# Experts' weights loaded in pairs of chunks, 2 MB at a time, for the 41st to the 180th chunk of each layer

## What is computed

```python
def moe(x, w_router, b_router, w1, w3, w2):      # per layer; 16 experts, top 2 of one group
    e_idx, gates = route(xf, w_router, b_router)
    ...
    def expert_block(args):
        xb, e = args
        hb = jax.nn.silu(xb @ w1[e]) * (xb @ w3[e])
        return hb @ w2[e]                        # w1, w3, w2: [2 layers, 16, 1024, 1024] float32
```

## Time and profile before

| | us |
|---|---|
| Median of 3 runs (1787.92 to 1788.83) | 1788.22 |
| Span of the profiled execution | 1787.6 |
| PE busy (share of the span) | 1720.1 (96%) |
| DVE busy | 790.6 (44%) |
| ACT busy | 624.1 (35%) |
| Queue of the weights, share of 16 DMA engines | 75.9% |
| Chain that ended last: PE, DMA | 71%, 17% |
| DMAs issued, all queues together (the view of DMA issues, added up) | 529 in number |

### The profile page before, as it was taken

The page is one execution under the profiler, slowest core; times in us unless marked ns, Lnnn a source line. Parts: engine busy times, 40 slices in busy tenths (PEclk is TensorE's granted clock), DMA queues, the critical chain, the costliest instruction groups (busy, mean ns, idle before and its releaser), DMA issues.

```text
span 1787.6 us, 24011 instructions
## 1 busy us (share of the span) xinstructions
PE 1720.1 (96%) x10024; PEld 1114.5 (62%) x10024; DVE 790.6 (44%) x1510; ACT 624.1 (35%) x1197; POOL 121.0 (7%) x143
## 2 busy tenths in 40 slices
PE   9999999999899989999999989999999999999998
PEld 8974344433234974444333333887999899789986
DVE  6961111111003782111111011866888677768875
ACT  5541110000002661000000001666666564656664
POOL 0000000000000000000000000131111001401100
PEclk9999999999999999999999999999999999999999
DMA  9569999999999779999999999543555544435550
GB/s 390 236 249 409 423 424 423 422 422 421 419 421 419 279 298 391 423 423 424 422 422 421 419 420 420 194 141 120 188 189 177 199 159 150 141 120 179 186 189 24
DMA packets 76100, 544.91 MB, mean 305 GB/s; under 512 B 8528, under 2 KB 8528, under 8 KB 10576
## 3 DMA queue, kind: packets, MB, share of 16 engines
q1 hardware_dynamic: 75600, 542.15, 75.9%
q10 hardware_dynamic: 384, 1.13, 0.2%
HBM read 542.19 MB, written 1.05 MB: 304 GB/s over the span
## 4 chain that ended last, share of the span: by engine, by line
PE 71%; DMA 17%; DVE 7%; ACT 3%; issue 1%; POOL 1%; SPq 0%; DVEq 0%; ACTq 0%
PE PS L1112 25%; DMA ring<-in_w 17%; PE PS L383 12%; PE PS L385 11%; PE PS L384 11%; PE PS L1092 2%; PE PS L1166 2%; DVE wl L366 2%; PE PS L834 1%; PE PS L593 1%; ACT wh L360 1%; PE PS L1128 1%; PE PS L1180 1%; PE PS L1275 0%; DVE F L969 0%
## 5 line engine op out<-in xcount | busy, mean ns | idle before, releaser
L1112 PE MATMUL PS<-ring,F 128*64 128x512 f32 x1992 | 454.4, 597 | 30.4 <-DMA ring<-in_w 22.8
L366 DVE TENSOR_TENSOR wl<-ring,wh 128x512 fp32r<-128x512 f32 x504 | 363.6, 740 | 167.7 <-ACT wh L360 165.1
L360 ACT ACTIVATE wh<-ring 128x512 fp32r<-128x512 f32 x504 | 314.5, 631 | 273.6 <-PE PS L385 257.6
L383 PE MATMUL PS<-xh,wl 128*128 128x256 f32 x1168 | 336.5, 288 | 2.4 <-DVE wl L366 2.3
L1112 PEld LDWEIGHTS PS<-ring,F 128*64 128x64 f32 x1992 | 136.9, 137 | 322.4 <-issue 252.6
L384 PE MATMUL PS<-xl,wh 128*128 128x256 f32 x1168 | 330.4, 283 | 0.0
L385 PE MATMUL PS<-xh,wh 128*128 128x256 f32 x1168 | 330.3, 283 | 0.0
L383 PEld LDWEIGHTS PS<-xh,wl 128*128 128x128 f32 x1168 | 223.9, 192 | 5.6 <-DVE wl L366 2.7
L384 PEld LDWEIGHTS PS<-xl,wh 128*128 128x128 f32 x1168 | 223.9, 192 | 0.6
L385 PEld LDWEIGHTS PS<-xh,wh 128*128 128x128 f32 x1168 | 223.9, 192 | 0.0
L383 PE MATMUL PS<-wh,xl 128*128 128x512 f32 x352 | 142.5, 405 | 6.4 <-DVE xl L500 3.5
(11 more groups left out here) (393 smaller groups left out, 1905.0 us busy)
## 6 DMA issues: line engine op xcount, KB each, us to landing
ring<-in_w SPq DMA_DIRECT2D x255, 1024.0 KB, 26.6
F<-in_w SPq DMA_DIRECT2D x56, 1024.0 KB, 23.1
ring<-in_ffn_up SPq DMA_DIRECT2D x44, 1024.0 KB, 4.9
early<-in_w SPq DMA_DIRECT2D x40, 1024.0 KB, 24.4
ring<-in_ffn_down SPq DMA_DIRECT2D x22, 1024.0 KB, 4.9
Z<-in_w SPq DMA_DIRECT2D x21, 1024.0 KB, 26.7
XT<-in_w SPq DMA_DIRECT2D x10, 1024.0 KB, 24.2
ring<-in_even_w_in SPq DMA_DIRECT2D x9, 1024.0 KB, 19.7
```

The source lines that it names most:

```text
L360: act.e.activation(self.wh[:, p % NPIECE, :], self.piece_source(p), ACT.Copy).then_inc(*self.up("w_hi", p))
L366: dve.e.tensor_tensor(self.wl[:, p % NPIECE, :], self.piece_source(p), f32(self.wh[:, p % NPIECE, :]), ALU.subtract).then_inc(*self.up("w_ ...
L383: e.matmul(out, left[1], right[0], start=first, stop=False)
L1112: t = pe.e.matmul(PS[64 * half:64 * half + 64, bank, :], lhs(k), weights[:, a:a + 512], start=(k == 0), stop=(k == 7))
```

## The change

Expert loads at positions 40 to 179 of a layer are made two chunks at a time: one DMA of 128 rows of 16 KB (2 MB) into two slots that lie side by side. To allow it:

- slots are dealt in fixed pairs there: six pairs of the ring, (13, 12) and (15, 14) in F, (17, 18) and (19, 20) in `early`, and (Z, XT), for which Z and XT become one buffer. Up to chunk 127 that is 11 pairs, 22 slots; from 128 to 179 the six pairs of the ring, 12 slots. The pair whose younger chunk is the oldest is taken;
- SP waits for the release of both old chunks before it issues; both new chunks count as landed with the one DMA's semaphore;
- in HBM the four chunks of a matrix are laid side by side, [128, 8192], so that two neighbouring chunks are one run of 16 KB a partition. A single chunk is then 128 rows of 8 KB, 32 KB apart.

Chunks 0 to 39 and 180 to 191 of a layer are loaded singly as before, and so is every other weight.

```diff
+GROUPS = {2: [(i, i + 1) for i in range(0, RING, 2)] + [(13, 12), (15, 14), (17, 18), (19, 20), (Z_SLOT, XT_SLOT)]}
+FIRST_OF, SIZE = [], {}
+def _load_size(i):
+    return 2 if 40 <= i < 180 else 1
+def _oldest(groups, last):
+    return min(groups, key=lambda g: max(-1 if last[x] is None else last[x] for x in g))
...
     for position, n in enumerate(LOAD_ORDER):
-        slots = [*range(RING), Z_SLOT] if n < CHUNK["aq0"] else list(range(SMALL_RING))
-        slot = None
+        if SLOT[n] is not None:
+            continue
+        slots, size, group = [*range(RING), Z_SLOT] if n < CHUNK["aq0"] else list(range(SMALL_RING)), 1, None
...
+            size = _load_size(i)
             if i < len(FIRST_SLOTS[layer]):
-                slot = FIRST_SLOTS[layer][i]
+                group = FIRST_SLOTS[layer][i] and (FIRST_SLOTS[layer][i],)
             elif i < 128:
                 slots += [*F_SLOTS, *SPLIT_SLOTS, XT_SLOT]
-        if slot is None:
-            slot = min(slots, key=lambda x: -1 if last[x] is None else last[x])
-        SLOT[n], PREVIOUS[n] = slot, last[slot]
-        last[slot] = n
-        loads[slot] += n > 0
-        LOADS[n] = loads[slot]
+        if group is None:
+            group = _oldest([g for g in GROUPS[size] if set(g) <= set(slots)] if size > 1 else [(x,) for x in slots], last)
+        SIZE[n] = size
+        loads[group[0]] += n > 0
+        for m, slot in enumerate(group, n):
+            assert LOAD_ORDER[position + m - n] == m
+            SLOT[m], PREVIOUS[m], FIRST_OF[m] = slot, last[slot], n
+            LOADS[m] = loads[group[0]]
+            last[slot] = m
...
-        self.Z = sb("Z", [128, NT, D])
-        self.XT = sb("XT", [128, KD, T])
+        self.ZX = sb("ZX", [128, 2 * CH])
+        self.Z = self.ZX[:, 0:CH].rearrange("p (h d) -> p h d", h=NT)
+        self.XT = self.ZX[:, CH:2 * CH].rearrange("p (k t) -> p k t", k=KD)
...
-            return A[("w1", "w3", "w2")[i // 4 % 3]][int(name[3]), i // 12, i % 4]
+            c = i % 4 * CH
+            return A[("w1", "w3", "w2")[i // 4 % 3]][int(name[3]), i // 12, :, c:c + SIZE[n] * CH]
...
     def landed(self, n):
-        return self.ring_sems[SLOT[n]], 16 * LOADS[n]
+        return self.ring_sems[SLOT[FIRST_OF[n]]], 16 * LOADS[n]
...
+            if FIRST_OF[n] != n:
+                continue
             if KIND[n] == "expert" and SLOT[n] >= RING:
                 sp.wait_ge(*self.extra_free(n))
-            if PREVIOUS[n] is not None:
-                sp.wait_ge(self.released(PREVIOUS[n]))
+            for m in range(n, n + SIZE[n]):
+                if PREVIOUS[m] is not None:
+                    sp.wait_ge(self.released(PREVIOUS[m]))
...
-                sp.e.dma_start(self.chunk(n)[:, 0:src.shape[-1]], src).then_inc(self.ring_sems[SLOT[n]], 16)
+                sp.e.dma_start(self.chunk(n, SIZE[n])[:, 0:src.shape[-1]], src).then_inc(self.ring_sems[SLOT[n]], 16)
...
-        a[k] = c(w.reshape(2, 16, 4, 2, 128, 1024).transpose(0, 1, 2, 4, 3, 5).reshape(2, 16, 4, 128, 2048))
-    by_columns = i["moe_w2"][:, 15].reshape(2, 2, 4, 128, 2, 512).transpose(0, 4, 1, 3, 2, 5).reshape(2, 4, 128, 2048)
+        a[k] = c(i[n].reshape(2, 16, 8, 128, 1024).transpose(0, 1, 3, 2, 4).reshape(2, 16, 128, 8192))
+    by_columns = i["moe_w2"][:, 15].reshape(2, 2, 4, 128, 2, 512).transpose(0, 3, 4, 1, 2, 5).reshape(2, 128, 8192)
```

More of the change, by code:

```diff
@@ L128, in _place_stream @@
     last, loads = [None] * (RING + EXTRA), [0] * (RING + EXTRA)
-    SLOT.extend([None] * len(KIND))
-    PREVIOUS.extend([None] * len(KIND))
-    LOADS.extend([None] * len(KIND))
+    for table in (SLOT, PREVIOUS, LOADS, FIRST_OF):
+        table.extend([None] * len(KIND))
     for position, n in enumerate(LOAD_ORDER):
-        slots = [*range(RING), Z_SLOT] if n < CHUNK["aq0"] else list(range(SMALL_RING))
-        slot = None
+        if SLOT[n] is not None:
+            continue
+        slots, size, group = [*range(RING), Z_SLOT] if n < CHUNK["aq0"] else list(range(SMALL_RING)), 1, None
         if KIND[n] == "expert":
@@ L253, in __init__ @@
         assert nc.sbuf_base <= split_at
[L255 to L258, removed]
+        ring, early = (t[:, :, :].rearrange("p r c -> p (r c)") for t in (self.ring, self.early))
+        self.places = [(ring, i * CH) for i in range(RING)] + [(self.F, 12672 - CH * i) for i in range(5)] + [
+            (early, i * CH) for i in range(4)] + [(self.ZX, 0), (self.ZX, CH), (self.F, 2304)]
         self.over = [dma_sem(f"s_over_{n}") for n in ("pe", "act", "dve", "w")]
@@ L291, in source, with chunk @@
         if name.startswith("moe"):
-            return A[("w1", "w3", "w2")[i // 4 % 3]][int(name[3]), i // 12, i % 4]
+            c = i % 4 * CH
+            return A[("w1", "w3", "w2")[i // 4 % 3]][int(name[3]), i // 12, :, c:c + SIZE[n] * CH]
         return tensors[name][order[name][i] if name in order else i]
-    def chunk(self, n):
-        return self.slots[SLOT[n]]
+    def chunk(self, n, size=1):
+        buffer, at = self.places[SLOT[n]]
+        return buffer[:, at:at + size * CH]
     def landed(self, n):
-        return self.ring_sems[SLOT[n]], 16 * LOADS[n]
+        return self.ring_sems[SLOT[FIRST_OF[n]]], 16 * LOADS[n]
     def released(self, n):
@@ L1614, in overflow_sync @@
                     e.wait_ge(s_pe, 4 * w + c + (1 if w == 2 else 0))
-                e.dma_start(wb, self.A[("w1", "w3", "w2")[w]][layer, expert, c].rearrange("a p n -> (a p) n")
-                            ).then_inc(s_w, 16)
+                e.dma_start(wb, self.A[("w1", "w3", "w2")[w]][layer, expert, :, c * CH:c * CH + CH].rearrange(
+                    "a p n -> (a p) n")).then_inc(s_w, 16)
     def overflow_tensor(self, h, by_columns):
@@ L2470, in dilated_views @@
         F = self.F
-        XF = self.XT[:, :, :].rearrange("p k t -> p (k t)")
-        ZF = self.Z[:, :, :].rearrange("p h d -> p (h d)")
+        XF = self.ZX[:, CH:2 * CH]
+        ZF = self.ZX[:, 0:CH]
         spare = self.ring[:, 7:10, :].rearrange("p r c -> p (r c)")
@@ L2897, in layout @@
     for k, n in (("w1", "moe_w1"), ("w3", "moe_w3"), ("w2", "moe_w2")):
-        w = i[n]
-        a[k] = c(w.reshape(2, 16, 4, 2, 128, 1024).transpose(0, 1, 2, 4, 3, 5).reshape(2, 16, 4, 128, 2048))
-    by_columns = i["moe_w2"][:, 15].reshape(2, 2, 4, 128, 2, 512).transpose(0, 4, 1, 3, 2, 5).reshape(2, 4, 128, 2048)
+        a[k] = c(i[n].reshape(2, 16, 8, 128, 1024).transpose(0, 1, 3, 2, 4).reshape(2, 16, 128, 8192))
+    by_columns = i["moe_w2"][:, 15].reshape(2, 2, 4, 128, 2, 512).transpose(0, 3, 4, 1, 2, 5).reshape(2, 128, 8192)
     a["w2"] = c(np.concatenate([a["w2"][:, :15], by_columns[:, None]], axis=1))
```

## The result

| | before | after |
|---|---|---|
| Median of 5 runs, us | 1788.35 | 1782.10 |
| Lowest to highest | 1787.92 to 1788.83 | 1780.29 to 1782.92 |
| Ratio, 95% interval | | 0.996 [0.9949, 0.9971] |
| Span of the profiled execution | 1787.6 | 1780.8 |

The kernel is 6.25 us faster by the medians, 6.8 by the profiled spans; the interval makes it 5.2 to 9.1 us. The forecast was 10.4. The direction was right and the size too large by 4 us.

What follows compares the result with a forecast made beforehand. DMA was taken to bound both expert stages, each layer ending when its bytes are in. Packet savings of 10.5 us less 0.1 for release gave 10.4 off 1788.2: 1777.8 us, own range 1776.0 to 1780.5, widened to 1776.0 to 1787.5.

Steps and rivals of the forecast that it cites:

- rival A: Expert loads: 16 KB rows still travel as 8 KB packets, so 1787.5 us; chance 0.12.
- Rival B: Reads from HBM: all engines together stop just above the highest slice, at 425 GB/s, so 1784.8 us; chance 0.10.
- The bound: Both expert stages: DMA at full share, each layer ends when its bytes are in; both layers' gains add up.
- The packets: Paired expert loads: 8.8 ns fixed cost per packet, 75 ns saved a pair, 10.5 us over two layers.
- the completion write: One fewer per pair on each engine: saves between 0 and 9 ns, included in the 75 ns a pair.
- The release term: Where pairs wait for two slots, tightest at the first pairs: queue not empty, 0.1 us put down for all.
- second tight pair: Pair (52, 53) of layer 1, waiting for chunk 34: covered by 0.9 us; the same assumed in layer 0.
- Landing of pairs at the end: Layer's end: 12 single chunks let PE catch up, cost 0; without them up to 1.7 us a layer.
- The layout: Expert chunks in HBM, rows 32 KB apart instead of 8 KB: taken as 0, bounds 0 to 9 us.
- Rival C: Expert loads: distance of the source rows slows HBM; 9 us eats the gain, twice that gives 1796 us; chance 0.12.

## Why the prediction was right and wrong

- **The number.** 1782.10 us lies outside the forecast's own range, 1776.0 to 1780.5. It lies in the stated range, 1776.0 to 1787.5, only because that had been widened for rivals A and B, and both fell. That the stated range held is luck; the direction is not.
- **The bound.** Right. Each layer ended with its bytes, and layer 0's gain was carried through the second mixer: PE begins on the last half chunk of layer 0 3.7 us earlier than before (559.82 for 563.52) and on that of layer 1 6.7 us earlier (1102.13 for 1108.87), and the span ends 6.8 us earlier. The forecast for the two places was 5.2 and 10.4.
- **The packets.** Right in mechanism and nearly in size. A pair was priced at 75 ns; pairs from the 65th chunk give 69 ns by the median, near 8.6 ns for each of 8 packets saved, and the 4 KB rows give 7.2, both in place of 8.8. The 5 ns in the 75 for the completion write are seen in no run. Over 140 pairs, 69 ns make 9.7 us in place of 10.5. The packet count fell as forecast, and rival A (rows sent as 8 KB) is ruled out by it. The stretches reached 426 to 428 GB/s where 427 to 430 was forecast.
- **The release term failed.** "The queue is just not empty: cost 0, with 0.3 us either way", and 0.1 us for all of it. Measured: 9.7 - 6.25 = 3.4 us by the medians, 2.9 by the spans, and 2.6 us by the rates where the pairs begin (0.7 in layer 0, 1.9 in layer 1). Waits in twos without the packet gain cost 1.7 and 1.6 us. The landings themselves were forecast well at the first place: shifted by the 3.7 us that layer 0 gained, chunk 39 was due at 724.4 and pair (40, 41) at 729.2; they came at 724.6 and 729.5. The error was to read the state of the queue from them. A landing is the last engine's; nine of the 16 were through with chunk 39 two us before it, and they had no work until the pair's first packets, which start at 722.97. The margins of 0.1 and 0.9 us that were computed were smaller than that spread. At the second place pair (52, 53) landed at 760.5 where 757.8 was worked out. And "I assume the same in layer 0" was wrong: layer 0 has no second tight pair.
- **Landing of pairs at the end.** Right: 12 single chunks were enough for pairs. In the changed kernel the last half chunk of layer 0 is there at 559.4 and PE begins on it at 559.8. Without that tail (pairs to the 190th chunk) PE is 1.8 us further behind its data in layer 0 and 0.6 in layer 1 than with pairs to the 180th, where up to 1.7 was forecast. The times, -6.4 us against -8.0 in two comparisons, point the same way but do not show it alone, since their intervals overlap.
- **The layout.** Right at 0. Rival C fell. The Trainium skill ("DMA: Bandwidth & Descriptors", Latency and other measured facts) warns of row pitches from 512 KiB on; at 32 KB the run with the layout alone shows no loss.
- **A wrong step without effect.** The prediction put 341 GB/s at 1 MB as following from 2.0 us plus bytes/436 GB/s. That sum is 4.4 us, or 238 GB/s; the Trainium skill ("DMA: Bandwidth & Descriptors", Bandwidth) has the 341 as a measured row, for DMAs issued from GpSimd. Nothing in the forecast rests on either.
- **Rival B**, the ceiling at 425 GB/s, fell: 431 was reached with 32 KB rows.

What stays open: the rates account for 2.6 of the 2.9 to 3.4 us; the rest is within the noise of the 69 ns. Why pair (52, 53) came 2.7 us after its worked-out landing is not shown. Landings of all these kernels also step by 0.5 to 1.5 us at single chunks or pairs, in the kernel before as well, but not at the same ones; the changed kernel has such a step in layer 1 at pair (48, 49), between the two places. Whether the engines that idled are those that were late there wasn't tried; the trace gives no engine for a packet.

## What to carry to other kernels

If a stage moves at the full share of the DMA engines, count its packets: here each cost some 6 to 9 ns beside its bytes, and longer contiguous rows in HBM and in SBUF removed them, while larger DMAs alone did nothing. Pay for longer rows with coarser releases and landings only where the queue is deep and the consumer has slack afterwards: begin them once some 20 us are queued (from the 65th chunk on a load landed 20 to 23 us after its issue, and nothing was lost), and end them early enough for the consumer to catch up. To see if a queue ran short, look for the place one us at a time, then compare the GB/s of a stretch of 20 us or more around it with a run that has no such place; landings do not show it.

## What the runs showed of the hardware that was not expected

- After a gap the first packets are slow. In the us from 181 and from 723, 16 KB packets took about twice their usual 0.61 us, so a gap costs more than its idle time.
- The 16 DMA engines drift apart in a long stream. For chunk 39 of layer 1 the first was through at 722.19 and the last at 724.64, in the kernel after; late in layer 0 of the kernel before the 16 ends of one chunk lie between 505.7 and 510.7, 5 us or two chunks apart.
- A packet of 32 KB still pays. The rates at a full share were 410 to 415 GB/s with rows of 4 KB, 420 to 423 with 8 KB, 426 to 428 with 16 KB and 427 to 431 with 32 KB.
- A start of pairs 12 chunks earlier, where one of them landed 7.3 us after its issue and not 20 or more, turned a gain of 6 us into a loss of 1.
